# Down weights of the routed experts loaded from ACT's queue instead of SP's, in a two-layer MoE kernel

## The reference, cut to what matters

```
scores = sigmoid(h @ router_w); idx = top_k(scores + router_bias, 8)
for each of 64 experts e, over the tokens routed to it:
    out = (silu(x @ w_gate[e]) * (x @ w_up[e])) @ w_down[e]      # 1024 -> 256 -> 1024
    result[token] += gate_weight * out
result += shared expert (dense)
```

## Time and profile before

| | |
|---|---|
| median of the runs | 3105.01 us (3 runs, 3105.0 to 3105.82) |
| profiled execution | 3093.14 us |
| span of the profiled execution | 3091.0 us |
| PE busy | 2580.1 us, 83% |
| DVE, ACT, POOL busy | 1242.6, 580.2, 567.8 us |
| moved | 573.17 MB |
| expert loop, layer 0 | from about 1000 to 1665 us |
| expert loop, layer 1 | from about 2450 to 3045 us |

### The profile page before, as it was taken

One profiled execution on the slowest core, in us unless ns is written; L12 is line 12 of the kernel. 1 busy time (PEld: TensorE's weight loads), 2 busy tenths in 40 slices (PEclk: granted clock), 3 DMA queues, 4 the chain that ended last, 5 costly groups with the idle time before them and its releaser, 6 DMA issues.

```text
span 3091.0 us, 44060 instructions
## 1 busy us (share of the span) xinstructions
PE 2580.1 (83%) x14904; PEld 1751.5 (57%) x14905; DVE 1242.6 (40%) x2705; ACT 580.2 (19%) x980; POOL 567.8 (18%) x561
## 2 busy tenths in 40 slices
PE   6999778778676999999996789777786699999985
PEld 3337667767563555555553445676675455555553
DVE  3432566666443222222222443456664322222223
ACT  1125211212110111111111115312211011111111
POOL 0000222222004222222221000122220222222221
PEclk8999878878778999999998799878788799999998
DMA  5643000000142899999997243100003499999994
GB/s 224 236 156 99 1 1 1 1 1 1 44 195 84 309 362 352 351 341 337 361 347 231 96 163 94 33 1 1 1 1 109 181 349 370 366 365 367 375 361 150
DMA packets 170445, 573.17 MB, mean 185 GB/s; under 512 B 31966, under 2 KB 81446, under 8 KB 131398
## 3 DMA queue, kind: packets, MB, share of 16 engines
q1 hardware_dynamic: 143718, 520.29, 44.4%
q0 software_dynamic: 26592, 51.11, 6.8%
HBM read 552.37 MB, written 53.53 MB: 196 GB/s over the span
## 4 chain that ended last, share of the span: by engine, by line
PE 55%; DVE 18%; DMA 12%; issue 6%; DVEq 3%; ACT 2%; POOLq 1%; POOL 1%; ACTq 1%; SPq 0%
PE ps L1552 50%; DMA featT<-ffn_rows,idx_in 8%; DVE R L983 7%; PE ps L1556 5%; DMA R<-in_exp_down 2%; DVE featT L983 1%; DVE R L989 1%; DMA R<-in_w_mod 1%; ACT L758 1%; ACT R L758 1%; POOLq L674 1%; DVE R L1299 1%; DVEq L980 1%; POOL slots L650 1%; DVE R L1198 1%
## 5 line engine op out<-in xcount | busy, mean ns | idle before, releaser
L1552 PE MATMUL ps<-R 128*64 128x256 f32 (+5 forms) x10224 | 1618.8, 382 | 165.6 <-DVE R L983 88.3
L1552 PEld LDWEIGHTS ps<-R 128*64 128x64 f32 (+2 forms) x10224 | 1052.8, 178 | 600.7 <-issue 319.3
L983 DVE TENSOR_TENSOR R<-R,ps 128x256 f32<-128x256 f32 (+2 forms) x364 | 216.2, 594 | 676.5 <-ACT R L758 500.8
L758 ACT ACTIVATE R<-ps 128x256 f32<-128x256 f32 (+2 forms) x387 | 164.2, 424 | 1163.6 <-PE ps L1552 1142.1
L1552 PE MATMUL ps<-featT,ring 128*128 128x512 f32 (+1 forms) x768 | 318.5, 573 | 1.6 <-ACT R L758 0.8
L1552 PEld LDWEIGHTS ps<-featT,ring 128*128 128x128 f32 x768 | 150.2, 199 | 165.6 <-issue 159.2
L1556 PE MATMUL ps<-ident,featT 128*128 128x128 f32 x1120 | 161.5, 290 | 91.0 <-DMA featT<-ffn_rows,idx_in 56.9
L986 DVE TENSOR_SCALAR R<-ps,idx_out 128x512 f32<-128x512 f32 x128 | 96.1, 751 | 300.1 <-PE ps L1552 300.1
L1556 PEld LDWEIGHTS ps<-ident,featT 128*128 128x128 f32 x1120 | 127.1, 146 | 147.1 <-issue 58.3
L640 POOL TENSOR_TENSOR R<-R,lev 128x512 f32<-128x512 f32 x112 | 142.5, 1272 | 346.1 <-PE ps L1552 218.7
L992 DVE COPY R<-ps 128x256 f32<-128x256 f32 (+2 forms) x282 | 154.3, 547 | 115.5 <-PE ps L1556 97.8
(11 more groups left out here) (183 smaller groups left out, 1540.2 us busy)
## 6 DMA issues: line engine op xcount, KB each, us to landing
R<-in_exp_gate SPq DMA_DIRECT2D x128, 1024.0 KB, 7.9
R<-in_exp_up SPq DMA_DIRECT2D x128, 1024.0 KB, 11.2
R<-in_exp_down SPq DMA_DIRECT2D x128, 1024.0 KB, 15.9
R<-in_w_mod SPq DMA_DIRECT2D x48, 1024.0 KB, 7.7
ring<-in_w_in SPq DMA_DIRECT2D x30, 1024.0 KB, 6.0
ring<-in_w_out SPq DMA_DIRECT2D x8, 1024.0 KB, 5.3
ffn_sum_odd<-zero SPq DMA_DIRECT2D x6, 512.0 KB, 7.3
ffn_rows<-X SPq DMA_DIRECT2D x6, 512.0 KB, 2.7
```

The costliest lines, as they stand in the source:

```text
L758: do(C.activation(out_, in_, func, **kw), name)
L983: do(V.tensor_tensor(out_, a, b, op), name)
L1552: return MM(out_, lhsT, rhs, start=start, stop=stop)
```

## The change

SP no longer issues the down weights inside the loop. It issues the down weights of the first four experts as before. From the fifth on, ACT issues them: after its wait for the down products of expert e and ahead of its half of the output of e, it issues the load of the down weights of expert e+4 into the same slot, with the same semaphore. The count that PE waits for is unchanged (48 for each expert).

```diff
@@ SP @@
                     sp.dma_start(flat(s, 1), up_w[:, one].rearrange("p e f -> p (e f)")).then_inc(S[f"w{s}"], 16)
-                    sp.dma_start(wdn[s][:, :, :], down_w[:, one].rearrange("p e k n -> p (e k) n")).then_inc(S[f"w{s}"], 16)
 
                 for s in range(NSLOT):
                     expert(s, s)
+                    sp.dma_start(wdn[s][:, :, :], down_w[:, s:s + 1].rearrange("p e k n -> p (e k) n")).then_inc(S[f"w{s}"], 16)
@@ ACT @@
+                down_w = A["exp_down"][l:l + 1].rearrange("o e (k p) n -> p (o e) k n", p=P)
+
                 def act_step(i, s, ahead):
...
                     act.wait_ge(S["dn_ps"], e + 1)
+                    if ahead > NSLOT:
+
+                        act.dma_start(wdn[s][:, :, :], down_w[:, bass.ds(i * NSLOT + (s + NSLOT), 1)].rearrange("p e k n -> p (e k) n")).then_inc(S[f"w{s}"], 16)
                     f(oe[s % 2][:, 0:512], ps[:, 4 + 2 * (s % 2), :], ACT.Identity, "oe_act", scale=idxS[s][:, 1:2])
```

## The result

The changed kernel takes **3169.31 us** (median of 4 runs, 3163.85 to 3175.54) where the kernel before takes 3105.41 us in the same comparison. The ratio is 1.0213 (95% interval 1.0201 to 1.0226), some 65 us slower. The prediction had the direction right and the size wrong (+27 us, 3132); the time is that of rival A. The profiled execution has a span of 3168.8 us against 3091.0; 14.5 of these 78 us lie ahead of the loop of layer 0, whose first down products end at 1029.1 us instead of 1014.6.

The account below looks back on a forecast made before the run. Expert loops were balanced between PE and DMA transfers, PE waiting on gather and weights. ACT's issue 11 us, gather's share 12 and near-bound gathers 4 made +27; profiled 3120 plus the runs' 11.9 gave 3132 us; range 3093 to 3178.

Parts of the forecast that it names:

- rival A: Gather starved: the second queue costs the gather 2 us or more in the expert loops; 3168 us; chance 0.19.
- The bound and the ring: Expert loops: PE and transfers balanced; scatter-gather ring 8.5 us per expert against PE's 8.3, so any delay comes out on PE.
- ACT's issue: Down-weight issue ahead of ACT's output: 0.5 us later scatter and gather, in 22 ring turns, 11 us.
- SP's lost issue: One down-weight issue per expert removed from SP, 0.38 us long, the last of its three: worth nothing.
- The order of the weights: Down moved to ACT's queue: down may land earlier, but the last of three weight landings stays put; value 0.
- the prediction's own sign: Landings in the expert loops: prediction is wrong if the last weight landing moves by more than 1 us.
- The gather's share: Gather beside two weight queues gets a third, not half: +0.75 us in layer 0, +0.36 in layer 1, 12 us.
- PE's own durations kept: Landings carried forward with PE's durations unchanged: +16 us in layer 0, +11 in layer 1; near-bound gathers add some 4.
- B: No difference: ACT's issue costs 0.3 us, gather's share unchanged, queues share the same 16 engines; 3109 us; chance 0.18.
- C: Faster: two queues bring the weight sets in sooner, worth at most 40 us of weight waits; 3095 us; chance 0.11.
- D: Change doesn't do what it says: ACT reaches its issue late, so down weights are late; slower; chance 0.02.

Follow-up runs that it names:

- experiment 4: The changed kernel (two weight queues) with the gather issued one expert earlier: 1.0012 against the kernel before.
- experiment 5: The kernel before (one weight queue) with the gather issued one expert earlier: 1.0011 against the kernel before.
- experiment 3: The kernel before with one extra ACT activation of 384 columns ahead of its output, queues unchanged: 1.0011, some 3.5 us.
- experiments 14 to 18: Gate or down on ACT's queue behind its output, piece lengths varied: 0.75 to 0.80% slower with 4 KB on SP's queue, up to 1.77% without; 18: one-queue control.
- experiment 6: The changed kernel with the gate weights instead of down on ACT's queue, ahead of ACT's output: 1.0113 against the kernel before.
- experiment 12: The changed kernel with down read in 8 KB pieces (another result, same amount of work): 1.0195 against the kernel before.

## Why the prediction was wrong in size

**The bound and the ring: right for after, half right for before.** The order of work in the gather ring was read rightly: experiments 4 and 5 take the gather off the path, and the loss is gone with it. But "any delay in it comes out on PE" does not hold for before. A turn of the ring is 8.5 us per expert, while the mean step of layer 1 is 9.1 us (580.4 / 64), and freeing the gather there gained nothing (1.0011, experiment 5): the transfers were the tighter bound in the mean.

**ACT's issue: nearly right in its size, not in its worth by itself.** It is 0.37 to 0.47 us long and lets the gather go 0.61 us later in the mean (forecast 0.5). What SP's lost issue is worth was not measured by itself. The forecast made 11 us of it; alone it is worth 3.5 us (experiment 3), because weight waits give way, and 17 us on top of a second queue.

**The order of the weights: wrong.** I left the last landing of a set where it was. It came 3.5 and 3.0 us sooner after the slot was free (13.6 and 13.5 us instead of 17.1 and 16.4), down itself about 12 us after its issue. By the prediction's own sign (the last landing moves by more than 1 us) this step failed. It is no gain of the second queue: at equal load the sets land no sooner with two queues (18.7 and 17.4 us, experiment 4) than with one (17.9 and 17.3 us, experiment 5). The steps of after are longer, so less stands in the queues, and PE no longer waits for weights. Rival A had named this, as what limits it.

**The gather's share: the first of the two steps that failed.** The term was +0.75 us in layer 0 and +0.36 us in layer 1, the data of the gather at a third instead of a half of the engines. The gathers of after took +0.63 and +1.00 us, and that in a loop whose load had already fallen (335 and 344 GB/s). At equal load it is +3.2 and +1.8 us (experiments 4 and 5), the "2 us or more" of rival A. The view that misled is the earlier trace rows: a latency of 7.9 us of which 4.5 come from load was priced by the 0.13 MB of the gather, when it goes by what stands beside it (experiments 14 to 18). (Nor is the gather "a thirtieth of the bytes": 0.131 of 3.15 MB is a 24th, and in layer 0 it is a 12th.) Of the two ends taken from the earlier trace rows, 0 and 4.5 us more, the measured +3.2 and +1.8 lie in the middle, and I had stayed near the low one.

**PE's clock: missing, the second and larger one.** Layer 0 shows it best. There the delays added up as forecast (0.61 + 0.63 = 1.24 us against 1.25), which is luck for the gather's part, as it stood beside a lighter load than the forecast had; and the gaps grew as forecast: 53.5 - 34.9 = 18.6 us against 16. The loop still grew by 34.0 us. The rest is PE itself, busy 15.6 us longer for the same work (slow groups +17.0): long waits for the gather, and a slower PE behind them. In layer 1 the gaps grew by 24.7 us (forecast 11, as its gather term was too small) and PE's busy time by 7.2 us (slow groups +10.1). Over both layers: gaps 43 us where the forecast had 27, and 23 us of slower PE for which it had no term; together that is the loops' 65.7 us. "PE's own durations kept" stood in the working as an assumption, and it was the costly one.

**The rivals.** A has the time (3168), but by luck, as its sum is another: the gathers of after were late by 0.63 and 1.00 us, not by 2, and the clock made up the rest. B falls, and with it, for this kernel, the rule of the Trainium skill, "DMA: Bandwidth & Descriptors", section "Issuing engines are not separate DMA queues", as I had put it. That no bandwidth is gained agrees with the runs; that nothing is lost, which was my conclusion and not the page's words, doesn't: the transfers share 16 engines, but a small transfer beside two queues lands 1.8 to 3.2 us later. C falls: the weight sets do land sooner and the weight waits are gone, to no use. D falls by the timeline.

**What stays open.** How an engine serves its queues was not seen, only its results: that SP's pieces count for the gather and ACT's hardly do is a finding from five kernels, without a mechanism. In experiment 6 the gather's mean latency is that of before and yet the loss is 1.1%; the wider spread goes with it, but what widens it is not shown. The effect of the clock was read from matmul durations and the granted clock, which agree; no run took it away by itself.

## What to carry to other kernels

Here a second queue brought no bandwidth to DMA engines that were occupied 0.97 to 0.99 of the time, and it made the small transfers beside it slower; if a loop turns on such a transfer, keep the bulk in one queue or issue the small one a step earlier, and if there must be two queues, try shorter pieces. A wait has a price only against the wait that would come next: the same 0.6 us cost 3.5 us where weights and gather traded, and 17 us where they didn't. Where data of one set are wanted at different times, one queue in the order of use and a semaphore for each use is worth more than a second queue, and a wait that grows on PE should be priced with the slower matmuls behind it.

## What the chip showed that I had not expected

- Two weight queues instead of one add 1.8 us (layer 1) and 3.2 us (layer 0) to a gather of 0.13 and 0.26 MB at the same throughput (364 and 367 GB/s in layer 1).
- The length of the pieces beside it matters to a gather even with one queue: 8.44 and 6.88 us beside 4 KB pieces, 9.98 and 8.03 us beside 8 KB pieces.
- Two queues with 8 KB pieces each get about equal shares (208 to 214 and 199 to 212 GB/s in experiment 12); 8 KB against 4 KB gets 1.7 to 1 (259 and 154 GB/s in after).
- After a wait of 5.94 us, 8 transposes took 1.97 us instead of 1.09 and 8 down products 4.37 us instead of 3.60.
